# The v projection in column groups of 1024 with five turns as seven block products, and loads issued when their place is free

## The reference, cut to what matters

```python
h = rmsnorm(x, a_norm)
z = h @ w_in                          # (256 x 2048) @ (2048 x 12288)
u, v, gate = jnp.split(z, 3, axis=-1)
u = gelu(u)
v = rmsnorm(gelu(v), v_gain)          # v: 4096 columns
sv = einsum('gpq,bnqgc->bnpgc', w_s, vc) + b_s   # per group, over 128 tokens
x = x + (u * sv * silu(gate)) @ w_out
# ... second block: attention, mLSTM, gates ...
x = x + (silu(u_gate) * u_val) @ w_down          # (256 x 5632) @ (5632 x 2048)
```

## Time and profile before

| | |
|---|---|
| runs | 2125.08, 2128.59, 2128.38 us, median 2128.38 |
| profiled execution | 2127.12 us, its span 2125.3 us |
| granted TensorE clock | 0.998 on average |
| DVE, ACT busy | 1313.1 and 1045.8 us |
| DMA | 404.37 MB, 190 GB/s on average |
| matmuls | 10090 |

### The profile page before, as it was taken

How to read it: one execution, slowest core, us unless ns; L and a number is a source line. 1 busy time by engine, 2 the same in 40 slices (tenths; PEclk the granted TensorE clock), 3 DMA queues, 4 the chain that set the end, 5 groups by cost and what they waited for, 6 DMA issues and landing times.

```text
span 2125.3 us, 24874 instructions
## 1 busy us (share of the span) xinstructions
PE 2116.2 (100%) x10090; PEld 1771.0 (83%) x10090; DVE 1313.1 (62%) x1466; ACT 1045.8 (49%) x1220; POOL 16.6 (1%) x17
## 2 busy tenths in 40 slices
PE   9999999999999999999999999999999999999999
PEld 7888888888888887888888888888888888887887
DVE  5445566656555554554654555567777777779984
ACT  6445444444444444554454444455555555555552
POOL 0000000000000000100000000000000000000000
PEclk9999999999999999999999999999999999999999
DMA  8665566555755555544455565556556556554554
GB/s 303 197 195 172 189 203 204 191 193 179 253 188 188 188 197 170 177 150 149 149 187 190 187 196 186 185 176 189 188 182 195 192 183 194 182 189 178 219 219 157
DMA packets 111810, 404.37 MB, mean 190 GB/s; under 512 B 12496, under 2 KB 13264, under 8 KB 111312
## 3 DMA queue, kind: packets, MB, share of 16 engines
q1 hardware_dynamic: 109440, 394.66, 56.3%
q10 hardware_dynamic: 2256, 8.14, 1.0%
HBM read 400.65 MB, written 2.10 MB: 189 GB/s over the span
## 4 chain that ended last, share of the span: by engine, by line
PE 94%; DVE 4%; DMA 1%; ACT 1%; issue 0%; SPq 0%; ACTq 0%; DVEq 0%
PE g L409 61%; PE xs L428 8%; PE g L428 8%; PE g L693 5%; PE xs L432 4%; PE g L432 4%; DVE w_lo L1090 2%; PE xs L452 1%; DMA raw<-in_stream 1%; PE xs L714 1%; DVE block L1094 1%; PE xs L573 1%; PE g L714 1%; PE xs L481 1%; ACT w_hi L764 0%
## 5 line engine op out<-in xcount | busy, mean ns | idle before, releaser
L1090 DVE TENSOR_TENSOR w_lo<-raw,w_hi 128x1024 fp32r<-128x1024 f32 x719 | 877.5, 1224 | 758.7 <-ACT w_hi L764 755.2
L764 ACT ACTIVATE w_hi<-raw 128x1024 fp32r<-128x1024 f32 x719 | 760.9, 1059 | 956.2 <-PE g L409 643.5
L409 PE MATMUL g<-w_hi,in_both 128*128 128x512 f32 x1536 | 478.5, 391 | 3.3 <-DVE w_lo L1160 3.3
L409 PE MATMUL g<-w_hi,mid_both 128*128 128x512 f32 x1280 | 406.5, 393 | 0.0
L409 PEld LDWEIGHTS g<-w_hi,in_both 128*128 128x128 f32 x1536 | 289.7, 189 | 63.7 <-DVE in_both L1153 3.5
L409 PE MATMUL g<-w_lo,in_both 128*128 128x512 f32 x768 | 299.8, 390 | 0.0
L409 PEld LDWEIGHTS g<-w_hi,mid_both 128*128 128x128 f32 x1280 | 240.4, 188 | 49.6
L409 PE MATMUL g<-w_lo,mid_both 128*128 128x512 f32 x640 | 249.2, 389 | 0.0
L428 PE MATMUL g<-mlp_both,w_hi 128*128 128x512 f32 x704 | 176.7, 393 | 0.4 <-DVE xw L1449 0.4
L428 PE MATMUL xs<-mlp_both,w_hi 128*128 128x512 f32 x704 | 176.3, 392 | 0.0
L409 PEld LDWEIGHTS g<-w_lo,in_both 128*128 128x128 f32 x768 | 144.9, 189 | 29.7
(11 more groups left out here) (263 smaller groups left out, 2049.8 us busy)
## 6 DMA issues: line engine op xcount, KB each, us to landing
raw<-in_stream SPq DMA_DIRECT2D x719, 512.0 KB, 3.5
block<-in_stream SPq DMA_DIRECT2D x24, 512.0 KB, 5.4
x_first<-in_x_tokens ACTq DMA_DIRECT2D x1, 2048.0 KB, 9.8
gain_row<-in_gain_rows SPq DMA_DIRECT2D x8, 256.0 KB, 2.7
xt<-in_x_tokens ACTq DMA_DIRECT2D x1, 2048.0 KB, 8.3
xf<-in_x SPq DMA_DIRECT2D x3, 512.0 KB, 9.3
out<-xw ACTq DMA_DIRECT2D x3, 512.0 KB, 3.1
final_row<-in_final_rows ACTq DMA_DIRECT2D x1, 1024.0 KB, 13.3
```

The lines of the kernel that those rows point to most:

```text
L409: ins = mm(G[buf][:, t, :], a[:, kt, at_t], w[:, slot, j * COLS:(j + 1) * COLS], start=(kt == 0 and n == 0), stop=(last and j == ROWS_PER_ ...
L764: activation(w_hi[:, n % RING, :], of[:], ACT.Copy).then_inc(hi_ready, 1)
L1090: v.tensor_tensor(w_lo[:, n % RING, :], of, w_hi[:, n % RING, :].bitcast(F32), ALU.subtract).then_inc(lo_ready, 1)
```

## The change

v gets the form that "down" has: four groups of 1024 columns with all four banks of `g`. Of its 16 turns (four of each group) five are done by products: two in group 1, one in group 2, two in group 3; the rest are plain. The groups have 16, 22, 19 and 22 items. Five turns take 7 x 6 matmuls in place of 4 x 12. The code for "down" and v is now shared (`Item`, `wide_chunk`, `wide_product`, `sums_of_rows`).

In v, group 0 has no products: ACT copies its results to `v_all` without gelu, as the scale of x isn't known yet, and does their gelu later (items 20 and 23). For groups 1 to 3, DVE adds the own products' sums to what is in `g` and writes `v_all` (`v_result`); ACT's gelu then works in place on `v_all`. Each gelu of a block of 512 columns is followed by its two sums of squares. The row sums of two turns (3 and 2) are kept for all groups.

Loads: SP goes through the items once; at an item it waits until the item's low half is made and issues the load that goes into the place that the item has left: the raw chunk four chunks on, and after the products 7, 3, 4 and 2 the block of the next turn by products (`NEXT_IN_PLACE`), for which three of the four block buffers change their roles from turn to turn (`buffer_of`). This holds for v and "down".

Start: 17 warm-up matmuls in place of 11, and the parts of x go one place earlier in SP's order from part 3 on; in ACT's and DVE's order the splits of x from part 2 on stand behind those of chunks 2 and 3.

The diff, cut to its core:

```diff
-WARM_UP = 11
+WARM_UP = 17
...
+WIDE_STEPS = {
+    "v": (((0, None), (1, None), (2, None), (3, None)),
+          ((0, 3), (1, 2)),
+          ((0, None), (1, 3), (2, None)),
+          ((0, 2), (1, 3))),
+    "down": (((3, None), (4, None), (8, None), (9, None), (5, 0), (6, 1), (7, 2), (10, None)),
+             ((3, 0), (4, 1), (5, 2), (6, None), (7, None), (8, None), (9, None), (10, None))),
+}
+SUM_TURNS = {"v": (3, 2), "down": (0, 1, 2)}
+SUMS_AT = {"v": (7, 10), "down": (7, 9, 11)}
+PLAIN = ("C0", "C1", "C2", "C3")
...
+NEXT_IN_PLACE = {7: B11, 3: B12, 4: B22, 2: B21}
...
+BLOCKS_AT = {FIRST_ITEM[_name] + _n: (_name, _b) for _name in WIDE_STEPS for _n, _b in ((6, B11), (7, B12), (9, B22), (10, B21))}
...
+def buffer_of(q, b):
+    return b if b == B21 else (b + q - quads_ahead(QUADS[q][0])) % 3
...
-            def load_chunk(c, of):
-                sp.wait_ge(lo_ready, CHUNK_ITEMS[c - RING] + 1)
-                sp.dma_start(raw[:, c % RING, :], stream[of]).then_inc(raw_full[c % RING], 16)
-            for c in range(RING, DOWN_AT):
-                load_chunk(c, c)
...
+            for n, item in enumerate(ITEMS):
+                if item.product in NEXT_IN_PLACE and quad_of(item) + 1 < len(QUADS):
+                    q = quad_of(item)
+                    if QUADS[q + 1][0] == item.phase:
+                        sp.wait_ge(lo_ready, n + 1)
+                        load_block(q + 1, NEXT_IN_PLACE[item.product])
+                if not item.product and CHUNK_COUNT[n] + RING < len(CHUNK_ITEMS):
+                    c = CHUNK_COUNT[n] + RING
+                    sp.wait_ge(lo_ready, n + 1)
+                    sp.dma_start(raw[:, c % RING, :], stream[stream_of(ITEMS[CHUNK_ITEMS[c]])]).then_inc(
+                        raw_full[c % RING], 16)
+                if n in BLOCKS_AT:
+                    phase, b = BLOCKS_AT[n]
+                    if phase == "down":
+                        sp.wait_ge(sem["f_lo_ready"], UP_TURNS)
+                    load_block(quads_ahead(phase), b)
...
-            for n, item in enumerate(DOWN):
-                if not item.product:
-                    load_chunk(CHUNK_COUNT[DOWN_AT + n], DOWN_AT + 22 * (2 * item.group + item.half) + item.row)
-                for b in LOADED_BEFORE.get(item.product, ()):
-                    g, i = item.group, item.turn
-                    if g == 0 and i == 0:
-                        sp.wait_ge(sem["f_lo_ready"], UP_TURNS)
-                    else:
-                        before = (g, i - 1) if i else (g - 1, BY_PRODUCTS - 1)
-                        sp.wait_ge(lo_ready, product_item(*before, LAST_USE[b]) + 1)
-                    half = 1 if b in (B12, B22) else 0
-                    row = 1 if b in (B22, B21) else 0
-                    sp.dma_start(blocks[b][:], stream[DOWN_AT + 22 * (2 * g + half) + 2 * i + row]).then_inc(
-                        block_full[b], 16)
...
+            def opens(item, bank):
+                key = (item.phase, item.group, bank)
+                new = key not in opened
+                if new:
+                    opened.add(key)
+                    _, _, read = group_of(item.phase, 2 * item.group + bank // 2)
+                    if read > 1:
+                        pe.wait_ge(group_read[bank // 2], read - 1)
+                return new
...
+            for n in range(items_of("v")):
+                item = ITEMS[n]
+                if n:
+                    pe.wait_ge(lo_ready, n + 1)
+                    if item.half == 0 and item.group == 0 and item.row:
+                        pe.wait_ge(sem["in_lo_ready"], (3, 4, 4, 5, 5, 6, 6)[item.row - 1])
+                if item.product:
+                    if item.product == 1:
+                        pe.wait_ge(sem["sums_lo_ready"], sum_slot("v", item.turn) + 1)
+                    ins = wide_product(item, norm_in.hi, norm_in.lo, n % RING)
+                else:
+                    ins = wide_chunk(item, norm_in.hi, norm_in.lo, n % RING)
+                ins.then_inc(mm_done, 1)
...
-            def v_out(g):
-                product, read, _ = done("v", g)
-                by_token(v_all[:, :, col_block(g)], product, ACT.Gelu_apprx_tanh, scale).then_inc(read, 1)
...
+                        if phase == "v":
+                            act.wait_ge(sem["x_sq_ready"], 2)
+                            act.wait_ge(group_read[0], g)
...
+            def v_taken(q):
+                product, read, _ = done("v", q)
+                activation(v_all[:, :, col_block(q)], product, ACT.Copy).then_inc(read, 1)
+            def v_out(q):
+                act.wait_ge(group_read[q % 2], q // 2 + 1)
+                at_v = v_all[:, :, col_block(q)]
+                by_token(at_v, at_v, ACT.Gelu_apprx_tanh, scale).then_inc(sem["v_ready"], 1)
+                act.wait_ge(sem["v_ready"], q + 1)
+                for t in range(2):
+                    ins = activation(v_junk[:, t, :], at_v[:, t, :], ACT.Square, accum_out=v_ss[:, t, q:q + 1])
+                ins.then_inc(sem["v_sq_ready"], 1)
+                act.wait_ge(sem["v_sq_ready"], q + 1)
...
+                first_product("v", n)
+                for q in range(7):
+                    if n == half_end("v", q // 2, q % 2) + 1:
+                        if q < 2:
+                            v_taken(q)
+                        else:
+                            v_out(q)
+                if n in (20, 23):
+                    if n == 20:
+                        act.wait_ge(sem["scale_ready"], 1)
+                    v_out((n - 20) // 3)
...
+                    if i == 0 and k == 0:
+                        v_out(7)
...
+            def own_products(n):
+                p1, u_a, u_b, u_d = v_wide.p1, v_wide.u_a, v_wide.u_b, v_wide.u_d
+                for g in range(1, 4):
+                    after = n - product_item("v", g, last_by_products("v", g), 6)
+                    if after == 0:
+                        dve.wait_ge(sem["p1_ready"], own_ahead("v", g) + 1)
+                        dve.wait_ge(mm_done, n + 1)
+                        link(v.tensor_tensor(u_a[:], XS[:, 2, :], p1[:], ALU.add))
+                    if after == 1:
+                        link(v.tensor_tensor(u_b[:], XS[:, 3, :], u_a[:], ALU.add))
+                    if after == 2:
+                        link(v.tensor_tensor(u_a[:], XS[:, 1, :], u_a[:], ALU.add))
+                    if after == 3:
+                        link(v.tensor_tensor(u_d[:], XS[:, 1, :], u_b[:], ALU.add))
+                        dve.sem_inc(sem["own_read"], 1)
+            def v_result(q):
+                half = q % 2
+                dve.wait_ge(mm_done, half_end("v", q // 2, half) + 1)
+                to = v_all[:, :, col_block(q)]
+                by_t = ((v_wide.p1, v_wide.u_b), (v_wide.u_a, v_wide.u_d))[half]
+                for t in range(2):
+                    ins = v.tensor_tensor(to[:, t, :], GG[:, 2 * half + t, :], by_t[t][:], ALU.add)
+                ins.then_inc(group_read[half], 1)
...
-            for buf in range(2):
-                dve.wait_ge(group_read[buf], 4)
-            link(v.tensor_tensor_reduce(y_lo[:, 0:16, :].rearrange("p a b -> p (a b)"), v_all[:, 1, :],
-                                        v_all[:, 1, :], scale=1.0, scalar=0.0, op0=ALU.mult, op1=ALU.add,
-                                        accum_out=v_stat[:, 1:2]))
...
+                own_products(n)
+                for q in range(2, 8):
+                    if n == half_end("v", q // 2, q % 2):
+                        v_result(q)
...
+                    if i == 0 and k == 1:
+                        dve.wait_ge(sem["v_sq_ready"], 8)
+                        link(v.tensor_reduce(v_stat[:, 0:2], v_ss[:], AXIS.X, ALU.add))
+                        mean_square(v_stat[:, 2:4], v_stat[:, 0:2], E).then_inc(sem["v_ms_ready"], 1)
+                    if i == 0 and k == 3:
+                        dve.wait_ge(sem["v_rstd_ready"], 1)
+                        dve.wait_ge(sem["ws_in"], 16)
...
```

More of the change, by code:

```diff
@@ L105 @@
+FIRST_ITEM["end"] = len(ITEMS)
+ITEM_AT = {item: n for n, item in enumerate(ITEMS)}
+CHUNK_ITEMS = [n for n, item in enumerate(ITEMS) if not item.product]
 CHUNK_COUNT = {n: c for c, n in enumerate(CHUNK_ITEMS)}
+QUADS = [(item.phase, item.group, item.turn) for item in ITEMS if item.product == 1]
+GROUPS_BY_PRODUCTS = list(dict.fromkeys(quad[:2] for quad in QUADS))
 B11, B12, B22, B21 = range(4)
 PRODUCT_OF = {1: B11, 5: B11, 7: B12, 6: B11, 3: B22, 4: B11, 2: B21}
-LAST_USE = {B11: 4, B12: 7, B22: 3, B21: 2}
@@ new lines, in banks_of, with half_end, stream_of @@
+def banks_of(item):
+    if item.product:
+        return {RESULT_OF[item.product]} if item.product in RESULT_OF else set()
+    return {2 * item.half, 2 * item.half + 1}
+def half_end(phase, g, half):
+    return max(n for n, item in enumerate(ITEMS) if (item.phase, item.group) == (phase, g) and
+               banks_of(item) & {2 * half, 2 * half + 1})
+def stream_of(item):
+    if item.group is None:
```

(4 more changed lines are left out.)

474 lines of the change are left out of this document (255 added, 219 removed).

## The result

The changed kernel takes 2132.69 us (median of 14 runs, 2130.39 to 2134.48), the kernel before 2126.39 (14 runs beside them, 2124.98 to 2128.76). The ratio is 1.0029, with a 95% interval of 1.0021 to 1.0037: slower, by 6.3 us. I had forecast 2126.3 with a range up to 2131.5, and 0.12 for slower. The profiled execution of after takes 2132.72 us (span 2130.9); the one of before took 2127.12 (span 2125.3).

What follows compares the result with a forecast made beforehand. PE's instruction stream plus its gaps was taken as the bound. From the profiled 2127.1 us, -6.8 + 4.6 + 4.7 - 1.7 - 2.2 = -1.4 gave 2125.7, and half of 1.3 carried over 2126.3; 8-in-10 range 2120.5 to 2131.5.

Steps and rivals of the forecast that it cites:

- Matmuls: In v, five turns by products save 30 matmuls at 0.2267 us each on PE: -6.8 us.
- (a) Handing over: After v's groups 1 and 3, PE waits for DVE's result before the banks open again: 2.28 us twice, +4.6 us.
- (b) Gelu and squares: In v, ACT's gelu and squares, and in group 3 also waits for DVE's result, make PE wait: +4.7 us.
- Loads in "down": In "down", each load goes out when its place is free, a turn earlier, removing later PE waits: -1.7 us.
- Start: At the start, six more warm-up matmuls cost nothing and the clock is full at 8.5 us: -2.2 us.
- Nothing late between the start and group 1: In v's group 0, plain items leave DVE free time that covers the row sums; the sum holds no PE wait there.
- The half of 1.3 us carried over to the median: Half of the 1.3 us between profiled execution and median was added to 2125.7, giving the forecast 2126.3 us.
- low clock: Rival for the start: half clock stays and the 2.2 us are not gained, 2128.5 us; chance 0.17.
- loads without effect: Rival for "down": DVE, not the late load, set the waits, so the 1.7 us are not gained, 2128; chance 0.06.
- lock: Rival for v: ACT and DVE wait for each other, six blocks pass 2.7 us each to PE, 16 us, 2137; chance 0.10.
- queues absorb it: Rival for v: five turns by products lose 0.4 us each, 2 us instead of 9.3, time 2119; chance 0.20.

Runs made afterwards that it cites:

- e11: e9 with the first hand-over (v_result of half group 2) put back behind DVE's last own sum and its low half: 2118.99 us, ratio 0.9969.
- e3: The changed kernel with DVE's sum that hands over a half group (v_result) ahead of the item's low half instead of behind it: 2126.14 us, ratio 0.9998.
- e5: e3 with the squares of half groups 0 to 5 two items behind their gelu instead of right behind it: 2125.23 us, ratio 0.9995.
- e8: The changed kernel with the edits of e1, e2 and e3, u_d behind the hand-over, group 0 copies earlier, gelu and squares apart: 2119.28 us, ratio 0.9967.
- e9: e8 with the load of x by token after item 9 instead of 4, and its squares and dependent gelus later: 2116.87 us, ratio 0.9954.
- e10: e9 with the four first block loads of v four items later as well: 2116.89 us, ratio 0.9954.
- e6: The changed kernel with ACT's gelu and squares of half groups 4 and 5 two and three items later, DVE's order unchanged: 2129.55 us, ratio 1.0017.
- e1: The changed kernel with the four first block loads of "down" issued four items later: 2130.23 us, ratio 1.0016.
- e2: The changed kernel without the wait for group_read[1] where "down" opens banks 2 and 3 of g: 2132.88 us, ratio 1.0033.
- e12: e9 with 11 warm-up products instead of 17: 2117.09 us, ratio 0.9956.
- e7: The kernel before with 17 warm-up products instead of 11: 2126.42 us, ratio 1.0006.
- e4: The changed kernel with 11 warm-up products instead of 17: 2133.11 us, ratio 1.0034.

## Why the prediction was wrong

It named the right places in v, and was wrong by 6.4 us, in these steps.

- *Matmuls, -6.8.* Right: 30 fewer at a pace that hasn't changed.
- *(a) Handing over, 2.28 twice = +4.6.* Right, with 2.39 and 2.77. What failed is the sentence that ends there: in some executions the first stand is also followed by a fall of the clock (0.50 granted from 100 to 102 us in after), which takes 1.68 us in the trace of after, and two executions of e11 take about 1.8 more at a lower mean clock. The prediction reckoned with the clock only at the start. Nine of after's 14 executions have a mean clock of 0.998 or 0.999 and a median of 2133.39, the five with 1.000 one of 2131.12; e3, e5, e8, e9 and e10, with stands of 1.5 us at most, have 36 executions, all 1.000.
- *(b) Gelu and squares, +4.7.* The size was right: 1.69 + 2.55 = 4.2, and the place of each wait. For group 3 the working had both causes in it, the work and the wait for DVE's result. e3 (work in its place, no wait) and e6 show that it was the second alone, so the 2.55 us of group 3 weren't a price of the work but of the order.
- *Loads in "down", -1.7.* **This step failed**: it became +1.6 between the two traces, and in no trace of after's loads does "down" come near the forecast. "Now each load goes out when its place is free, a turn earlier" is true from the second turn on, and the four later pairs are gone as forecast (1.7 us). It is not true of the first turn. Its loads moved from behind item 15 to behind item 6, ahead of f_low, and the raw loads behind them in SyncE's queue wait along. The prediction had read this mechanism in the earlier trace rows and not asked for it at the new place. e1 undoes it: 2.75 us. The other 1.2 are the wait for group_read[1], which before stood only at the first product of "down" and now stands at item 2 as well (e2, e8). With these 3.3 us gone, "down" comes out at the forecast: 0.63 us in e8, where the prediction left 0.6.
- *Start, -2.2.* **This step failed too.** No run shows this term, a gain of 2.2 us from 17 warm-up products in place of 11. The clock was full at the start in all eleven traces with 17 products (from the second matmul on the starts are 0.22 to 0.24 us apart), but x landed early in all of them and e12 has full clock with 11, so that no trace shows what keeps it up. Between the two profiled executions the price looks right as well, -0.8 - 1.1 = -1.8 (unrounded). But e7, the kernel before with 17 products, isn't faster (1.0006). And the runs of the kernel before in which the mean clock was 0.999 have a median only 0.5, 0.7, -0.1 and 0.9 us above those with 1.000, in the four sets of runs beside the experiments. And low halves are late at full clock: in e7 the waits for them take as much as the slow matmuls do in before (2.89 and 2.81 us).
- *Nothing late between the start and group 1.* Overlooked: +1.0 at 54 to 56, where PE waits for ACT's copy of group 0. Before, PE took the other pair of banks there. ACT stands behind x's two squares there (1.9 us each) and has had late chunks before them; e9 has moved both together and has no wait, which of the two it was isn't shown.
- *The half of 1.3 us carried over to the median.* It had no ground: after's runs spread as wide, and the median of before's 14 runs lies 0.7 us below its profiled execution, not 1.3 above.

The sum with measured terms, in the order matmuls, start, hand-overs, clock, gelu and squares, wait at 54, "down", small starts, is -6.8 - 1.8 + 5.2 + 1.7 + 4.2 + 1.0 + 1.6 + 0.5 = +5.6, from the profiled 2127.1 to that of after, 2132.7. The largest error is "down", 3.3 us, then the clock behind the hand-over, 1.7, then the wait at 54, 1.0. The rivals: "low clock" (half clock at the start, its 2.2 us not gained, 2128.5) and "loads without effect" (2128) stood nearest in time from below, but their reasons didn't hold: the clock was full at the start of after (1.00 granted from 8 to 9 us), and the loads had an effect of either sign. The "lock" of ACT and DVE exists, in one of its places, with 2.5 us and not 16; "queues absorb it" is what e9 gets by another order: all 30 matmuls gained (its "down" begins 8.4 us earlier than before's) and 1.8 us more in "down".

## What to carry to other kernels

When a change moves a load on an in-order queue, look up for every load at its new place what it waits for there and which loads stand behind it; a load that can go earlier may hold back those that were on time (here SyncE issued nothing from 1904.7 to 1914.52 us, and e1 gives back 2.75). When two engines feed each other item by item, put what hands over a resource (a bank, an input of the other engine) ahead of the bulk work of the same step: here that one place in the order was worth 6.6 us of the median, nearly as much as the 30 matmuls saved (6.8). And a gain that only one profiled execution shows, as the clock at the start, should be asked of the spread of the runs before it goes into a sum.

## What the runs showed of the hardware

- A stand of PE of 2.39 us at 96.6 us, after a stretch in which it was busy for 29.95 of 31 us (after, 65 to 96), was followed by starts 0.427 us apart for 3.4 us, at a granted clock of 0.50, in some executions and not in others with the same order of instructions there: in the traces of after, e1 and e4 yes, in those of e2 and e6 no, nor behind the 2.61 us of e11. The stand of 2.66 us at 186 was followed by it in none of these. What tells them apart stays open; I didn't test it. The number of slow matmuls at the start differs too between the three traces with 11 warm-up products, each of another kernel: 12 starts 0.427 us apart in before, 7 in e4, none in e12.
- After a wait the second matmul starts 0.08 to 0.12 us late as well, at nearly every wait of every trace here. A wait of 0.15 us, as the one at 149.7, costs 0.26 in all.
- At a granted clock of 0.50 the starts of the 128x512 matmuls are 0.427 us apart (before, 9.06 to 14.18 us), at 1.00 0.2267 (156 in 35.36 us).
- In the first microseconds the DMA engines bring 381 to 434 GB/s (the windows 8 to 9 and 12 to 13 us of before, e4, e7, e9 and e12), and the first real matmul starts at 7.52, 8.46 and 8.50 us with 11 warm-up products and between 7.51 and 7.96 with 17, each time after x has landed. Full clock at the start was no gain by itself in e7 (ratio 1.0006 against before): PE there waits for low halves, 2.89 us up to 45 us, where before has 2.81 of slow matmuls.
